# Experts' rows scattered in two halves of 512 columns into two tensors

## What is computed

```python
def expert_block(args):
    e, tok_b, wt_b = args
    xb = h_pad[tok_b]
    return swiglu(xb, w_gate[e], w_up[e], w_down[e]) * wt_b[:, None].astype(h.dtype)

yb = lax.map(expert_block, (block_e, tok.reshape(n_blocks, DISPATCH_BLOCK), wt.reshape(n_blocks, DISPATCH_BLOCK)))
return jnp.zeros((n + 1, d), h.dtype).at[tok].add(yb.reshape(-1, d))[:n]
```

## Time and profile before

| | |
|---|---|
| median of 3 runs | 2255.45 us |
| profiled execution | 2259.32 us |
| span of its instructions | 2257.3 us |
| TensorE matmuls busy | 2147.0 us, 95% |
| TensorE weight loads busy | 1836.2 us, 81% |
| VectorE busy | 1225.4 us, 54% |
| ScalarE busy | 1007.9 us, 45% |
| GpSimd busy | 497.1 us, 22% |
| granted TensorE clock, mean | 0.977 |
| DMA, experts' stage | busy share 0.8 to 0.9, some 280 GB/s |

### The profile page before, as it was taken

How to read it: one execution, slowest core, us unless ns; L and a number is a source line. 1 busy time by engine, 2 the same in 40 slices (tenths; PEclk the granted TensorE clock), 3 DMA queues, 4 the chain that set the end, 5 groups by cost and what they waited for, 6 DMA issues and landing times. The chain is left out here.

```text
span 2257.3 us, 41201 instructions
## 1 busy us (share of the span) xinstructions
PE 2147.0 (95%) x11538; PEld 1836.2 (81%) x11539; DVE 1225.4 (54%) x1999; ACT 1007.9 (45%) x1773; POOL 497.1 (22%) x540
## 2 busy tenths in 40 slices
PE   5999899999999989998979999999999899999888
PEld 3767559999999989997868888888888788877663
DVE  3624673112232332116776675777777677777765
ACT  3403793211111121113433665677776577667652
POOL 2400000000000000000001344455554344444235
PEclk8999899999999999999988999999999999999999
DMA  7360201112111001125322888899899899989876
GB/s 293 118 246 9 97 1 56 37 46 66 46 47 46 28 22 44 46 98 198 119 81 99 297 243 266 243 298 300 287 299 307 269 299 302 290 274 293 305 223 215
DMA packets 147804, 386.67 MB, mean 171 GB/s; under 512 B 21837, under 2 KB 86293, under 8 KB 123173
## 3 DMA queue, kind: packets, MB, share of 16 engines
q1 hardware_dynamic: 117764, 307.15, 37.6%
q0 software_dynamic: 29808, 78.05, 14.8%
q10 hardware_dynamic: 176, 0.75, 0.1%
HBM read 349.48 MB, written 70.07 MB: 186 GB/s over the span
## 5 line engine op out<-in xcount | busy, mean ns | idle before, releaser
L2085 PE MATMUL ex_pgu<-ex_wgu_hi,ex_xT_hi 128*128 (+1 forms) x784 | 314.6, 401 | 7.2 <-DVE ex_xT_lo L2255 6.7
L2243 DVE TENSOR_TENSOR ex_wgu_lo<-ex_stage_gu,ex_wgu_hi (+1 forms) x252 | 292.0, 1221 | 52.8 <-ACT ex_wgu_hi L2162 52.8
L2085 PE MATMUL ex_pgu<-ex_wgu_hi,ex_xT_lo 128*128 (+1 forms) x784 | 307.9, 393 | 0.0
L2085 PE MATMUL ex_pgu<-ex_wgu_lo,ex_xT_hi 128*128 (+1 forms) x784 | 307.1, 392 | 0.0
L2162 ACT CAST ex_wgu_hi<-ex_stage_gu (+1 forms) x252 | 245.6, 1047 | 50.2 <-DMA ex_stage_gu<-in_w_exp_up 29.4
L2002 POOL DMA_INDIRECT sum_rows<-ex_y,ex_index_scatter x98 | 170.1, 1736 | 413.5 <-issue 296.5
L981 PE MATMUL cv_ph<-fourth_r,cv_split 128*128 128x352 f32 (+1 forms) x1152 | 222.0, 327 | 2.1 <-DVE cv_split L1027 2.1
L1622 POOL MEMSET ex_rows<- 128x1088 f32 x1 | 1.0, 1004 | 947.8 <-ACT third_r L1594 947.8
L981 PEld LDWEIGHTS cv_ph<-fourth_r,cv_split 128*128 128x128 f32 x1152 | 196.0, 189 | 2.2 <-DVE cv_split L1027 2.2
L2085 PEld LDWEIGHTS ex_pgu<-ex_wgu_hi,ex_xT_hi 128*128 128x128 f32 x784 | 148.5, 189 | 37.9 <-issue 8.1
L2104 PE MATMUL ex_py<-ex_wdn_hi,ex_hT_hi 128*128 x392 | 164.3, 419 | 12.7 <-DVE ex_hT_lo L2268 12.7
(11 more groups left out here) (352 smaller groups left out, 4202.2 us busy)
## 6 DMA issues: line engine op xcount, KB each, us to landing
ex_stage_gu<-in_w_exp_gate SPq DMA_DIRECT2D x64, 1024.0 KB, 7.2
ex_stage_gu<-in_w_exp_up SPq DMA_DIRECT2D x64, 1024.0 KB, 10.5
ex_stage_dn<-in_w_exp_down SPq DMA_DIRECT2D x64, 1024.0 KB, 8.0
front_room<-in_w_ada SPq DMA_DIRECT2D x26, 512.0 KB, 5.7
w_ahead<-in_w_in SPq DMA_DIRECT2D x24, 512.0 KB, 3.9
third<-in_w_ada SPq DMA_DIRECT2D x16, 512.0 KB, 8.8
early_late<-in_w_in SPq DMA_DIRECT2D x16, 512.0 KB, 3.9
front_room<-in_w_in SPq DMA_DIRECT2D x3, 2048.0 KB, 12.6
```

Of the source, the lines that this page charges most:

```text
L2085: last = pe.matmul(pgu[:, :], xT[a][:, k, :], w, start=(k == 0 and (a, c) == PASSES[0]), stop=(k == KT - 1 and (a, c) == PASSES[-1]))
L2243: dve.tensor_tensor(gu_piece(1, slot, q), gu_raw(slot, q), gu_piece(0, slot, q).bitcast(F32), ALU.subtract).then_inc(gu_lo, 1)
```

## The change

`sum_rows` becomes two tensors of (1088, 512), left and right. `scatter` issues two indirect DMAs of 512 columns, first the left, then the right. Each waits for the landing of the same half of the block in front, and for its own half of `y`. There are four `y_stored` semaphores in place of two. ScalarE's copy of a half waits for the landing of the same half two blocks back. The zero stores and the loads of the sums are 18 each in place of 9, with half the bytes.

```diff
-            self.sum_rows = nc.dram_tensor("sum_rows", (TOK, D), F32, kind="Internal").ap()
+            self.sum_rows = [nc.dram_tensor(f"sum_rows_{n}", (TOK, D // 2), F32, kind="Internal").ap() for n in ("left", "right")]
...
-                    for t in range(NT):
-                        R = rows_of(t)
-                        sp.dma_start(self.sum_rows[t * P:t * P + R, :].rearrange("r (a n) -> r a n", n=256),
-                                     zero[:R, :].unsqueeze(1).to_broadcast([R, D // 256, 256])).then_inc(zeroed, 16)
-                    sp.wait_ge(zeroed, 16 * NT)
+                    for half in self.sum_rows:
+                        for t in range(NT):
+                            R = rows_of(t)
+                            sp.dma_start(half[t * P:t * P + R, :].rearrange("r (a n) -> r a n", n=256),
+                                         zero[:R, :].unsqueeze(1).to_broadcast([R, D // 512, 256])).then_inc(zeroed, 16)
+                    sp.wait_ge(zeroed, 16 * 2 * NT)
...
-        rows_gathered, y_stored = self.rows_gathered, [self.kept_sem(f"ex_y_stored{i}") for i in range(2)]
+        rows_gathered, y_stored = self.rows_gathered, [[self.kept_sem(f"ex_y_stored{i}{n}") for n in ("l", "r")] for i in range(2)]
...
-                        sp.dma_start(sums[t][:R, :], self.sum_rows[t * P:t * P + R, :]).then_inc(sum_loaded[t], 16)
+                        for j in range(2):
+                            sp.dma_start(sums[t][:R, j * 512:(j + 1) * 512], self.sum_rows[j][t * P:t * P + R, :]).then_inc(sum_loaded[t], 16)
...
-                        wait(y_stored[1 - o], landed_before)
-                        wait(y_ready, value)
-                        pool.indirect_dma_start(self.sum_rows, bass.IndirectOffsetOnAxis(ap=ixy[o][:, 0:1], axis=0),
-                                                y[o][:, :, :].rearrange("p a n -> p (a n)"), None,
-                                                bounds_check=TOK - 1, oob_is_err=False,
-                                                compute_op=ALU.add).then_inc(y_stored[o], 16)
+                        for j in range(2):
+                            wait(y_stored[1 - o][j], landed_before)
+                            wait(y_ready, value + (j - 1))
+                            pool.indirect_dma_start(self.sum_rows[j], bass.IndirectOffsetOnAxis(ap=ixy[o][:, 0:1], axis=0),
+                                                    y[o][:, j, :], None,
+                                                    bounds_check=TOK - 1, oob_is_err=False,
+                                                    compute_op=ALU.add).then_inc(y_stored[o][j], 16)
...
-                    wait(y_stored[0], m * 16 + 16)
-                    wait(y_stored[1], m * 16 + 16)
+                    for j in range(2):
+                        wait(y_stored[0][j], m * 16 + 16)
+                        wait(y_stored[1][j], m * 16 + 16)
...
-                        pool.wait_ge(sum_loaded[t], 16)
+                        pool.wait_ge(sum_loaded[t], 32)
...
                     def y_out(o, b, landed):
-                        act.wait_ge(y_stored[o], landed)
                         for j in range(2):
+                            act.wait_ge(y_stored[o][j], landed)
                             act.wait_ge(down, b * 2 + (j + 5))
                             act.copy(y[o][:, j, :], py[j][:, :]).then_inc(y_ready, 1)
```

More of the change, by code:

```diff
@@ L1872, in experts @@
             eps = sb("cb_eps", [P, 1])
-            landed = sb("ex_landed", [1, 2])
+            landed = sb("ex_landed", [1, 4])
             pt = [ps(f"ex_pt{i}", [P, 4, P]) for i in range(2)]
@@ L2022, in _ @@
                     for o in range(2):
-                        pool.dma_start(landed[:, o:o + 1], self.h2_rows[0:1, 0:1]).then_inc(y_stored[o], 16)
+                        for j in range(2):
+                            pool.dma_start(landed[:, 2 * o + j:2 * o + j + 1], self.h2_rows[0:1, 0:1]).then_inc(y_stored[o][j], 16)
                     pool.memset(eps[:, :], EPS).then_inc(eps_set, 1)
```

## The result

The changed kernel takes 2288.1 us, the median of 4 runs (2277.76 to 2293.22), against 2256.4 before: 1.0133 times as long, 95% interval 1.011 to 1.0155. Measured again later it was 1.0144 (1.0117 to 1.0171). It is slower by some 30 us where 11.5 us faster was forecast, and the time lies outside the range (2231 to 2272). Rival A was the right case, past the price it was given.

What follows compares the result with a forecast made beforehand. Bound by chained scatter landings (9.75 us per block against TensorE's 9.40) in the middle, by transfers late. Chain -12, DMA work +3, end -2.5 give -11.5 us: 2255.45 to 2244.0 us, range 2231 to 2272.

Steps and rivals of the forecast that it cites:

- Rival A: Slower: right half's landing behind gather and left half in one queue, and GpSimd's loop, lengthen the period; 2269, chance 0.28.
- What bounds the kernel before: Middle of the experts' stage: scatter landings chained at 9.75 us per block against TensorE's 9.40, 20 us of stalls.
- GpSimd's loop: GpSimd's turn per block with two scatters: 7.3 to 10.4 us, midway 8.9, hidden under TensorE's 9.40, charged nothing.
- The half's landing: Scatter of a right half: 8.72 less 0.85 for fewer bytes plus 0.7 for queueing behind the left, 8.57 us.
- -12 us for the chain: Middle stretch: with the shorter period, 8 us of TensorE's 20 us of stalls stay, a gain of 12 us.
- The chain's period: Time from one block's scatter to the next: falls from 9.75 to 9.60 us, ends 8.1 and 11.4.
- DMA work: Twice the scatter packets cost 10% more, 0.23 us per block; +3 us in the 12 transfer-bound late blocks, at most +28.
- The end: After the last blocks: halves in step take 3 us off the closing chain, more loads add 0.5; together -2.5 us.
- Zeroing: Nine more zero stores on SP fit into its wait of 81.4 us for TensorE; cost 0.
- The rule on round-robin queues: DMA engines alternate between queues packet by packet, so more, smaller scatter packets wait for more weight-packet turns; no separate size.

Runs made afterwards that it cites:

- the fills: The kernel before, with two fills of a scratch tile (128x1000) on GpSimd behind each scatter, some 1.9 us: 1.0011, 2259.7 us.
- the alternating tensors: The kernel before, even and odd blocks added into two tensors, each scatter waiting only two blocks back: 0.9892 with odd rows left out, 0.9965 complete.

## Why the prediction was wrong

- **What bounds the kernel before** was right. The chain's 9.75 us against TensorE's 9.40 made the stalls; with the chain gone, TensorE's count from 1300 to 2080 us rises from 3719 to 3821 instructions, and the time falls by 1.1%. The step from one turn to all of them, "landing plus 1.03 us is a period", was loose: 24 of the 84 scatters were released by ScalarE's copy of `y` and not by a landing.
- **GpSimd's loop** is the step that failed: "Midway is 8.9 us, so I charge nothing for it". The work of a turn wasn't set too low: it is 8.1 us on average, 6.5 to 10.9. The 2.26 us from gather to scatter, read as "nothing to wait for", even held 0.9 us of waiting (its pause is 1.19 us, the shortest are 0.3), which takes the ends to some 6.4 and 9.5. The error was to weigh the loop and the chain each by its own mean and take the larger. They lie in one order: GpSimd's work, then a wait for a landing, then the work again, and the gather behind all. Before, 3.7 us of waiting per turn absorbed everything else. Now 1.9 are left beside 8.1 of work, in two waits, and the turns in which a landing is late add to turns which are long anyway: 8.1 alone is under TensorE's 9.40, and the sum of the two is 9.98. The runs show it from three sides: work without a wait costs 0.1%, a second scatter that isn't awaited 0.3%, one that is awaited 1.3%; and with the loop shortened the waits are harmless (1.0025). Work as long as the changed kernel's (7.8 us with the fills, 8.0 with the scatter that isn't awaited) did next to no harm without the second landing's wait, so it takes both.
- **Rival A** named "the larger of two varying times" and gave it 0.28. It had the place, but its price of 2269 us was 19 us short; at the period that was measured, 9.98 us, its own sum gives 2276, and at 10.1 it had 2285.
- **The half's landing**: 8.57 us was forecast for the right, the median is 9.1; for the left 8.4. The saving of 0.85 us didn't appear at the median: two halves in flight landed as late as one whole row. The 0.7 us for a half in front, at most 1.7, was small beside the 3.9 between left and right in the run where each half waits for both. The term of the sum that rested on this, -12 us for the chain, is the second that failed: even with GpSimd's loop shortened on both sides the whole change gave 3.7 us. ScalarE's waits on scatters didn't fall either: 17.8 us from 1700 us on, as before.
- **The chain's period**: 9.60 forecast, 9.98 measured. With the prediction's own sum, (9.98-9.75) x 81 = +19 us, which is what the middle lost. That is the same loss counted another way, not a cause.
- **DMA work**: 10% more for the scatter was assumed, 0.23 us of every engine per block, +3 us late. The software queue takes 35.4% of 817 us for 82 blocks, 3.53 us of every engine per block. The same row of the kernel before, 1255 to 2072 us:

```profile
q0 software_dynamic: 24192, 64.63, 34.8%
```

  That is for 84 blocks, 3.38 us: 0.15 us more per block, gathers and all. An up matrix lands in 11.2 us from 2096 to 2169 us, 11.4 before. The middle's 19 us and the 4.8 in front make up the spans' whole difference, so nothing is left for the late stretch and the +3 was too much.
- **The end**: -2.5 forecast, 0 measured. The last `ex_y` copy ends at 2227.12 us, 53.9 us ahead of the span's end, as before (2203.42 of 2257.3). The last scatter follows it 1.4 us sooner (6.1 for 7.5 us), but from there to the first product it is 9.9 us where it was 7.3:

```profile
2233.22 1.55 POOL L2005 DMA_INDIRECT sum_rows_right<-ex_y,ex_index_scatter  x1 [0.69 <-issue]
2243.14 2.34 POOL L2067 TENSOR_TENSOR cb_room<-cb_room,ex_stage_dn 128x1024 f32<-128x1024 f32 x1 [8.37 <-DMA cb_room<-sum_rows_right]
```

- **Zeroing** cost nothing that can be seen, as said.
- **The rule on round-robin queues** that was cited for rival A (the Trainium skill, "DMA: Bandwidth & Descriptors", Queues, rings and completion order) is neither shown nor excluded: 128 more packets per block cost at most the 0.3% of the run with the scatter that isn't awaited, and that holds their descriptors too. But those packets were empty.

What stays open: how the 0.3% divides between descriptors and packets, why two copies of one column on VectorE cost 7 to 9 us, and why GpSimd's three small copies start 0.1 us apart in some turns and 1.1 in others, some 2 us of the spread of its work. It was not tried to have the halves in step with the alternating tensors.

## What to carry to other kernels

Where one engine both issues transfers and waits for them in order, a wait is paid by everything queued behind it; before adding a second one, write that engine's turn as a sum, its work and its waits in series, and ask what leaves last in it. To cut a chain of landings, remove the dependence (another destination) rather than cut the transfer: two halves in flight landed as late as one whole row, and doubled the issues. A cost of zero for an engine with slack holds only while its work and its waits do not have to fit into the same turn.

## What the runs showed of the hardware

- An accumulating indirect scatter with 128 indices landed after 8.6 us at the median with 4 KB rows, one in flight, and after 8.5 with 2 KB rows, two in flight, beside the weights' loads. Issued with no other scatter in flight, and at 234 to 253 GB/s where it was 269 to 281, a left half took 5.0.
- 128 indices out of bounds, with no byte moved, occupied GpSimd 1.55 us and more, as full rows do. Awaited one per block, such a scatter slowed the kernel by 1.3%; awaited two blocks later, by 0.3%.
- With scatters in flight that nobody has to wait for, each took longer (10.3 and 11.2 us) while the core moved more, 308 GB/s from 1700 to 2080 us for 290 before.
